# Two joined transformer blocks: narrower recurrence levels, query norms in pieces, and a pooling chain moved from GpSimd to VectorE

## The chip, the cores and the metric

The kernel runs on one NeuronCore of a Trainium2 chip. Its engines are TensorE (PE, matrix products), VectorE (DVE), ScalarE (ACT), GpSimd (POOL) and SyncE (SP, which here only issues DMAs). Each engine works through its own instruction list, and semaphores tie the lists together. The metric is the device time of one execution in microseconds; lower is better.

## The reference

Two models are computed, both with sequence 512 (S) and width 1024 (D). The first has two layers, each of mixer, cross-attention to a memory of 256 rows, and convolutional FFN. The even mixer joins a retention half and a gated recurrence half (HGRN2); the odd one is a dilated attention. The second has two equal layers of three parallel branches (attention with forget gates, short convolution, window pooling), gated and summed, and an FFN.

```python
# recurrence of the even mixer, per chunk (HGRN2)
cum = jnp.cumsum(lfn, axis=2)
w = jnp.exp(jnp.where(causal, cum[:, :, :, None, :] - cum[:, :, None, :, :], -jnp.inf))
scores = jnp.sum(qn[:, :, :, None, :] * kn[:, :, None, :, :] * w, axis=-1)
...
# cross-attention: both q and the memory's keys are normalised per head
q = _rms(_split_heads(h @ w_q, XA_HEADS), q_norm_g)
mk = _rms(_split_heads(mk, XA_HEADS), k_norm_g)
p = jax.nn.softmax(jnp.einsum('bhqd,bhkd->bhqk', q, mk) * (XA_HD ** -0.5), axis=-1)
o = jnp.einsum('bhqk,bhkd->bhqd', p, mv)
...
# pooling branch of the second model, windows 2, 4, 8, 16, one group of 64 channels each
cs = jnp.cumsum(uf, axis=1)
groups.append((csg - lagged) / counts - uf[:, :, sl])
out = jnp.einsum('bsgc,gcd->bsgd', d, w_grp).reshape(Bsz, S, D_MODEL)
```

## The kernel before

Activations stay in SBUF, transposed: 128 channels on the partitions, 512 positions along the row. Weights stream from HBM in units of 128x2048 floats (`raw`, two buffers, SP's queue). So that f32 weights can go through the PE fast and yet precisely, ACT writes a rounded copy of each unit, `wH` (L1197), and DVE the rest, `wL` = raw - wH (`split`, L1614). Activations are split likewise into `hH` and `hL`. Every product is then three matmuls (`passes`, L443): hH by wH, hL by wH, hH by wL. PE waits for `wl_ready`, SP may refill `raw` after it.

PE's work is counted in jobs: two PSUM tiles of `G` (four banks, so two jobs are open at a time). `job_done` tells DVE or ACT to read one, `job_free` gives the banks back. `psS` and `psT` (two banks each) serve scores, statistics and transposes. Nothing is scheduled at run time: the order on each engine is written out by hand, and each list blocks at its first unmet semaphore. DVE therefore is a strict queue in which weight splits, softmax rows and reads of finished jobs alternate.

What the change touches, by place:

- The recurrence levels (PE L782, DVE L2121 to L2140). The triangle of scores within a chunk is built in levels. At each level and for each of four heads PE multiplies keys by 512 query columns into psS; at level 0 DVE multiplies by a mask (L2137), at levels 1 to 5 it lets `copy_predicated` (L2140) take those entries that belong to the level, which all lie in the later half of each block. `grow` (L2121, L2122) prepares the next level's operands.
- The memory (ACT L1213 squares, PE L494 sums). Before each cross-attention ACT issues a DMA of the memory and directly waits for it, squares it and the residual stream in 128x512 pieces, and PE sums the squares over channels with a vector of ones.
- Cross-attention (PE L982, L989; DVE L2237 to L2275). Four query jobs are projected; after the last of them the squared queries of all four heads are summed (L499, L503), DVE copies 16 columns of sums out of PSUM (L1657), POOL raises them to -1/2 (L2511, 128x16) and 16 score rows start. A row: scores on PE, row maximum on DVE (L1821), times the norm (L2273), exponential on ACT (L1482), division on DVE, transpose and second product on PE.
- Dilated attention (PE L916, L933, L946; DVE L1821, L2186, L2213). 32 rows with value projections between them; `value_half` reads a projected tile and then splits the next weight unit (L1614).
- Second model's attention (PE L1080, L1089, L1116; DVE L2333, L2336, L1821, L2427, L2428). 32 rows in 16 pairs. Between them PE projects values, conv and pooling inputs; their squares and sums (L506) and DVE's reads (L2364, L2370, L2375) lie in the same lists. POOL meanwhile builds the window sums (L2587 to L2599) from position s=12 on. Four pool jobs follow at its end, each read by DVE (L2449) after a gate job (L1726).

`s_` and `d` below count the rows and the pairs of rows on which the three engines' lists are aligned.

## Time and profile before

| | us |
|---|---|
| median of 3 runs | 3182.88 (3181.28 to 3187.2) |
| profiled execution, device time | 3179.84 |
| its span (first to last instruction) | 3178.0 |
| PE busy | 3118.1 |
| DVE busy | 1584.6 |
| ACT busy | 1076.7 |
| POOL busy | 281.8 |
| mean granted PE clock | 0.992 |

A busy share is an average over stages. "Idle before" in a row is the time in which that engine did nothing before the instruction, with the engine and line that ended it behind the arrow. The ends of matmuls are modelled, so that durations of neighbouring matmul rows overlap; the distance of their starts is their cost.

### The profile page before, as it was taken

How to read it: one execution, taken by the hardware profiler on the slowest of the kernel's cores; microseconds unless marked ns; L12 is line 12 of the kernel's file. 1: busy time of each engine (PE TensorE's matmuls, PEld its weight loads, DVE VectorE, ACT ScalarE, POOL GpSimd, SP SyncE). 2: the span in 40 equal slices, each digit the busy share in tenths (PEclk: the TensorE clock that was granted, in tenths of full speed). 3: DMA queues.
4: the chain of work that ended last, by engine and by line, in shares of the span. 5: the costliest groups of instructions: out<-in, count | busy, mean ns of one | idle time of the engine just before them, and what ended most of it. 6: DMA issues, size and time to landing. Idle time of an engine off the chain costs nothing.

```text
span 3178.0 us, 38774 instructions
## 1 busy us (share of the span) xinstructions
PE 3118.1 (98%) x15548; PEld 2603.7 (82%) x15548; DVE 1584.6 (50%) x1852; ACT 1076.7 (34%) x1167; POOL 281.8 (9%) x161
## 2 busy tenths in 40 slices
PE   9999999999999899999999999999999999999998
PEld 7798988888889798888888778888888777888887
DVE  7574545554325554455435754544334765444433
ACT  3223334443223443444323332333322332233322
POOL 0002100110000020010001200111000200100100
PEclk9999999999999999999999999999999999999999
DMA  4411412222321131222233122222222222222223
GB/s 168 112 54 67 146 40 93 92 100 104 123 97 67 42 145 54 80 94 104 94 110 109 54 93 93 93 96 100 95 106 92 90 74 100 93 93 96 99 103 112
DMA packets 47721, 299.92 MB, mean 94 GB/s; under 512 B 7091, under 2 KB 7347, under 8 KB 13284
## 3 DMA queue, kind: packets, MB, share of 16 engines
q1 hardware_dynamic: 42480, 288.01, 25.7%
q10 hardware_dynamic: 5108, 10.02, 1.4%
q8 instruction: 98, 1.61, 0.2%
q14 instruction: 35, 0.29, 0.0%
HBM read 293.26 MB, written 4.75 MB: 94 GB/s over the span
## 4 chain that ended last, share of the span: by engine, by line
PE 90%; DVE 5%; ACT 2%; issue 2%; DMA 0%; POOL 0%; DVEq 0%; ACTq 0%; SPq 0%
PE G L443 82%; ACT wH L1197 1%; DVE wL L1614 1%; PE psS L782 1%; DVE mxt L1821 1%; PE psS L503 1%; PE psS L982 1%; PE G L989 1%; DVE ws L2336 1%; PE psS L1080 1%; PE G L1089 1%; DVE ws L2333 0%; PE psT L535 0%; PE psT L1116 0%; PE G L1007 0%
## 5 line engine op out<-in xcount | busy, mean ns | idle before, releaser
L443 PE MATMUL G<-hH,wH 128*128 128x512 f32 x2560 | 1019.9, 398 | 20.4 <-DVE ws L2364 5.7
L443 PE MATMUL G<-hH,wL 128*128 128x512 f32 x2560 | 1001.9, 391 | 0.0
L443 PE MATMUL G<-hL,wH 128*128 128x512 f32 x2560 | 1001.0, 391 | 0.0
L1614 DVE TENSOR_TENSOR wL<-raw,wH 128x2048 fp32r<-128x2048 f32 x265 | 637.5, 2406 | 647.3 <-ACT wH L1197 646.9
L443 PE MATMUL G<-wsr,wH 128*128 128x512 f32 (+1 forms) x2528 | 750.7, 380 | 1.4 <-DVE wsr L2202 0.9
L1197 ACT ACTIVATE wH<-raw 128x2048 fp32r<-128x2048 f32 x265 | 505.5, 1908 | 587.7 <-PE G L443 567.8
L443 PEld LDWEIGHTS G<-hH,wH 128*128 128x128 f32 x2560 | 483.6, 189 | 136.8 <-issue 17.6
L443 PEld LDWEIGHTS G<-hH,wL 128*128 128x128 f32 x2560 | 482.9, 189 | 103.2
L443 PEld LDWEIGHTS G<-hL,wH 128*128 128x128 f32 x2560 | 483.7, 189 | 99.5 <-issue 2.2
L443 PEld LDWEIGHTS G<-wsr,wH 128*128 128x128 f32 x2528 | 466.2, 189 | 94.8 <-DVE wsr L2202 1.8
L443 PE MATMUL G<-wsr,wL 128*128 128x512 f32 (+1 forms) x1264 | 479.0, 379 | 0.0
L443 PEld LDWEIGHTS G<-wsr,wL 128*128 128x128 f32 x1264 | 238.2, 188 | 44.6
L2533 POOL TENSOR_TENSOR wsr<-sq,wsr 128x1024 f32 x44 | 105.8, 2405 | 841.0 <-ACT wsr L1314 841.0
L2511 POOL TENSOR_TENSOR rsb<-ms,neghalf 128x4 f32<-128x4 f32 (+4 forms) x21 | 37.6, 1790 | 1144.4 <-DVE ms L1657 983.0
L1314 ACT ACTIVATE wsr<-sq 128x1024 f32 x44 | 46.7, 1061 | 231.5 <-DVE sq L1844 231.5
L1283 ACT ACTIVATE ws<-ws,mxt 128x128 f32<-128x128 f32 (+3 forms) x96 | 54.0, 563 | 206.7 <-DVE mxt L1821 206.1
L1768 DVE TENSOR_TENSOR x<-x,G 128x1024 f32<-128x1024 f32 x39 | 47.6, 1221 | 150.2 <-PE G L443 150.2
L443 PE MATMUL G<-wH,hH 128*128 128x256 f32 x384 | 112.1, 292 | 0.0
L443 PE MATMUL G<-wL,hH 128*128 128x256 f32 x384 | 108.6, 283 | 0.0
L443 PE MATMUL G<-wH,hL 128*128 128x256 f32 x384 | 108.5, 283 | 0.0
L1726 DVE TENSOR_TENSOR sq<-G,hmask 128x1024 f32<-128x1024 f32 x44 | 53.7, 1221 | 90.3 <-PE G L443 90.1
L1726 DVE TENSOR_TENSOR tn<-G,hmask 128x1024 f32<-128x1024 f32 x44 | 53.9, 1225 | 86.9 <-PE G L443 86.2
(275 smaller groups left out, 2570.2 us busy)
## 6 DMA issues: line engine op xcount, KB each, us to landing
raw<-in_units SPq DMA_DIRECT2D x265, 1024.0 KB, 4.8
ws<-bias_rows SPq DMA_DIRECT2D x2, 1536.0 KB, 14.9
bias_rows<-ws ACTq DMA_DIRECT2D x1, 2560.0 KB
x<-in_x SPq DMA_DIRECT2D x4, 512.0 KB, 7.4
ws<-in_mem ACTq DMA_DIRECT2D x2, 1024.0 KB, 5.0
ws<-bias_rows ACTq DMA_DIRECT2D x1, 2048.0 KB, 8.2
out_x<-x SPq DMA_DIRECT2D x4, 512.0 KB, 7.9
ws<-in_decay ACTq DMA_DIRECT2D x1, 1280.0 KB, 8.0
```

What stands on the lines that cost most here:

```text
L443: mm = pe.matmul(o, mv if swap else wt, wt if swap else mv, start=first and n == 0, stop=last and n == 2)
L503: mm = pe.matmul(st[:, col:col + 1], lhs, ones[:, 0:1], start=True, stop=True)
L782: mm = pe.matmul(psS[:, n % 2, o:o + w], k_[:, ks:ks + P], q_[:, qs:qs + w], start=True, stop=True)
L982: mm = pe.matmul(psS[:, r % 2, 0:M], ws[:, XQ + 2 * h + t, qt * P:qt * P + P], kx[:, 2 * h + t, :], start=(t == 0), stop=(t == 1))
L1197: activation(wH[:, g.p, :], raw[:, g.p, :], ACT.Copy).then_inc(wh_ready, 1)
L1283: return activation(p_, p_, ACT.Exp, bias=mxt[:, r % 4:r % 4 + 1], accum_out=den[:, r % 4:r % 4 + 1])
L1314: activation(aH[:, bass.ds(i * 2, 2), :], sq[:, 1], ACT.Copy).then_inc(ffn_h, 1)
L1614: V.tensor_tensor(wL[:, g.p, :], raw[:, g.p, :], wH[:, g.p, :].bitcast(F32), ALU.subtract)\
L1726: V.tensor_tensor(dst, g, rb_pair, ALU.mult).then_inc(job_free, 1)
L1768: V.tensor_tensor(x[:, 2 * jj:2 * jj + 2, :], x[:, 2 * jj:2 * jj + 2, :], g, ALU.add)\
L2511: W.tensor_tensor(dst[:, 0:cols], ms[:, 0:cols], neghalf[:].to_broadcast([P, cols]), ALU.pow)\
L2533: W.tensor_tensor(aL[:, bass.ds(i * 2, 2), :], sq[:, 1], aH[:, bass.ds(i * 2, 2), :].bitcast(F32), ALU.subtract).then_inc(ffn_ready, 1)
```

## The change

1. Recurrence. At levels 1 to 5 PE reads only the later half of each block's query columns, so 80 matmuls have 64 columns in place of 128 (128 for 256 in pairs), and DVE's `copy_predicated` moves 256 elements a row with strides in place of 512. The weight split that stood before level 0 is cut into four of 128x512 and put behind the four heads of level 1.
2. Memory. ACT issues the first memory DMA after its copies for the recurrence's last level, the second at row 20 of the dilated attention.
3. Cross-attention, both layers. The query norm is in four pieces of 4 columns (`query_norm`), so POOL raises 128x4 four times. Key scaling of the fourth head, the fourth query read, two of the norms and a weight split move from before the rows to between rows 0 and 4; the fourth sum goes to a `G` bank after score 1. ACT loads its table for the exponential in the third query step, and its rounding of one unit moves to row 3.
4. Dilated attention. Three weight splits move two rows down.
5. Second model, both layers. The window sums move from POOL to DVE, in six pieces at s=17, 19, 21, 23, 25 and 27 (`pooled`), with the final low parts between two gate jobs (`pooled_low`). The second half-statistics move from s=10 to s=13 and into another bank. The second and third pool job write to psS and psT, idle by then, and the weight splits stand after the first and the last pool read.

On DVE, at the recurrence's levels 0 and 1. Before:

```order
L1614 TENSOR_TENSOR wL<-raw,wH 128x2048 [waits wh_ready]
L2137 TENSOR_TENSOR ws<-psS,hmask 128x512 [waits hs_done] x4
L2121 TENSOR_TENSOR ws<-ws 128x64x4 [waits hz_ready,hs_done]
L2122 TENSOR_TENSOR ws<-ws 128x64x4
L2140 COPY_PREDICATED ws<-hmask,psS 128x512 [waits hm_ready]
```

and now, where L2173 is the old L2137, L2157 and L2158 `grow`, L2182 the narrower copy and L2144 a piece of the split:

```order
L2173 TENSOR_TENSOR ws<-psS,hmask 128x512 [waits hs_done] x4
L2157 TENSOR_TENSOR ws<-ws 128x64x4 [waits hz_ready,hs_done]
L2158 TENSOR_TENSOR ws<-ws 128x64x4
L2182 COPY_PREDICATED ws<-hmask,psS 128x64x4 [waits hm_ready]
L2144 TENSOR_TENSOR wL<-raw,wH 128x512 [waits wh_ready]
```

The split of 2048 columns has left the place ahead of the mask products and comes in quarters behind each head of level 1.

On DVE, from the last query job to the second row of a cross-attention. Before:

```order
L2258 TENSOR_SCALAR ws<-G,gqk 128x512 [waits sq_ready,job_done]
L2258 TENSOR_SCALAR ws<-G,gqk 128x512
L1614 TENSOR_TENSOR wL<-raw,wH 128x2048 [waits wh_ready]
L2265 TENSOR_TENSOR ws<-ws,psT 128x512 [waits rb_ready]
L1657 TENSOR_SCALAR ms<-psS 128x16 [waits sq_used]
L1821 TENSOR_REDUCE mxt<-psS 128x1 [waits s_done,rs_ready]
L2273 TENSOR_TENSOR mxt<-mxt,rsq 128x1 [waits dve_chain]
```

and now, where L2308 scales keys, L2315 copies sums out for POOL, L1846 and L2336 are a row's maximum and its norm, and L2302 reads queries:

```order
L2308 TENSOR_TENSOR ws<-ws,psT 128x512 [waits rb_ready]
L2315 TENSOR_SCALAR ms<-psS 128x4 [waits sq_used]
L1846 TENSOR_REDUCE mxt<-psS 128x1 [waits rs_ready,s_done]
L2336 TENSOR_TENSOR mxt<-mxt,rsq 128x1 [waits dve_chain]
L2308 TENSOR_TENSOR ws<-ws,psT 128x512 [waits rb_ready]
L1846 TENSOR_REDUCE mxt<-psS 128x1 [waits s_done]
L2336 TENSOR_TENSOR mxt<-mxt,rsq 128x1 [waits dve_chain]
L1835 RECIPROCAL rden<-den 128x1 [waits p_exp]
L1836 TENSOR_SCALAR ws<-ws,rden 128x256 [waits dve_chain]
L2315 TENSOR_SCALAR ms<-G 128x4 [waits sq_used]
```

The first row stands ahead of the fourth head's keys, queries and split; these come later, one to a row.

On DVE, at the end of the second model's attention, gates and pool jobs. Before:

```order
L1726 TENSOR_TENSOR ws<-G,hmask 128x1024 [waits job_done]
...
L1614 TENSOR_TENSOR wL<-raw,wH 128x2048 [waits wh_ready]
...
L1726 TENSOR_TENSOR ws<-G,hmask 128x1024 [waits job_done]
...
L2449 SCALAR_TENSOR_TENSOR ws<-G,pc,ws 128x512 [waits act_read]
L2449 SCALAR_TENSOR_TENSOR ws<-G,pc,ws 128x512
```

and now, where L1750 reads a gate, L2530 makes the low parts of the window sums and L2568 reads a pool job:

```order
L1638 TENSOR_TENSOR wL<-raw,wH 128x2048 [waits wh_ready]
L2530 TENSOR_TENSOR wsr<-sq,wsr 64x1024 [waits pdh_ready]
L2530 TENSOR_TENSOR wsr<-sq,wsr 64x1024
...
L1750 TENSOR_TENSOR ws<-G,hmask 128x1024 [waits job_done]
...
L2568 SCALAR_TENSOR_TENSOR ws<-psS,pc,ws 128x512 [waits act_read]
L2568 SCALAR_TENSOR_TENSOR ws<-psS,pc,ws 128x512
...
L2568 SCALAR_TENSOR_TENSOR ws<-psT,pc,ws 128x512 [waits act_read]
L2568 SCALAR_TENSOR_TENSOR ws<-psT,pc,ws 128x512
```

POOL's two last instructions of the window sums have become DVE's, and two pool reads come from psS and psT.

The diff, cut:

```diff
@@ attention of block 1, PE
-                pe.wait_ge(ms_ready, c.stat.v)
+                pe.wait_ge(ms_ready, keys_read + 2)
+                last_query = c.job.v + 2
                 for s_ in range(rows + PV_LAG):
                     if s_ < rows:
+                        if s_ == 12:
+                            pe.wait_ge(last_ready, l + 1)
+                            pe.wait_ge(job_free, last_query)
                         wait(pe, scores_read, c.row.v + (s_ - 1))
                         score(s_).then_inc(s_done, 1)
+                    if s_ == 1:
+                        stats("pair", 3, st=G[:, c.job.p * 2 + 1, :])
...
@@ recurrence, PE and DVE
+                                if 0 < lev < 6:
+                                    o, w, q = o // 2, w // 2, blocks(q, 2 ** (lev + 1))[1]
...
-                    step(inputs(1))
+                    step(inputs(1), unit=False)
+                    def split_part(q):
+                        at = slice(q * 512, q * 512 + 512)
+                        ins = V.tensor_tensor(wL[:, g.p, at], raw[:, g.p, at], wH[:, g.p, at].bitcast(F32), ALU.subtract)
...
+                                    b = psS[:, n % 2, 0:256].rearrange("p (k n l) -> p k n l", k=4, l=2 ** (lev + 1))
+                                    ins = V.copy_predicated(d, mask, b)
+                            if lev == 1:
+                                split_part(h)
@@ memory, ACT
-                    act.dma_start(memt[mem], a["mem"]).then_inc(mem_in, 16)
                     act.wait_ge(mem_in, 16 * (mem + 1))
...
+                    act.dma_start(memt[0], a["mem"]).then_inc(mem_in, 16)
                     step()
...
+                        elif s_ == 20:
+                            act.dma_start(memt[1], a["mem"]).then_inc(mem_in, 16)
@@ cross-attention, DVE
+                def between(s_):
+                    if s_ == 0:
+                        dve.wait_ge(rb_ready, c.bc.v)
+                        key_scale(3).then_inc(last_ready, 1)
+                    elif s_ == 1:
+                        query_norm(2)
+                    elif s_ == 2:
+                        step(queries(3), unit=False)
+                    elif s_ == 3:
+                        query_norm(3)
+                    elif s_ == 4:
+                        split()
+                        c.sq.off += 4
@@ second model, PE
-                    elif s_ == 10:
+                    elif s_ == 9:
+                        key_norm()
+                    elif s_ == 11:
                         pe.wait_ge(kn_read, (c.lay.v - 2) * 2 - 1)
-                        stats("half", 0, npairs=1, st=G[:, 3, :])
-                    elif s_ in (9, 11):
                         key_norm()
+                    elif s_ == 13:
+                        pe.wait_ge(pv_free, c.pv.v + 1)
+                        stats("half", 0, npairs=1, st=G[:, 1, :])
...
-                for jj in range(4):
-                    take_job()
+                for jj, bank in enumerate((None, psS, psT, None)):
+                    if bank is None:
+                        take_job()
...
+                    else:
+                        mm.then_inc(pooled_done, 1)
@@ second model, DVE
-                    elif s_ == 11:
-                        rstd_part(G[:, 3, :])
                     elif s_ == 12:
                         half_keys(1)
                         half_scaled(1, PX_)
+                    elif s_ == 15:
                         rstd_part_scaled(rsq[:, 16:32])
+                    elif s_ in (17, 19, 21, 23, 25, 27):
+                        pooled((s_ - 17) // 2)
...
+                def window(dst, src, lag):
+                    c.link(V.tensor_tensor(dst[:, :, lag:S], src[:, :, lag:S], src[:, :, 0:S - lag], ALU.add))
+                    c.link(V.tensor_copy(dst[:, :, 0:lag], src[:, :, 0:lag]))
+                def pooled(n):
+                    if n == 0:
+                        dve.wait_ge(pinv_in, (c.lay.v - 2) * 16)
+                        window(pa, u, 1)
...
+                    else:
+                        c.link(V.tensor_tensor(start, start, ws[rows, PINV:PINV + 2, 0:16], ALU.mult))
+                        V.tensor_tensor(start, start, u[rows, :, 0:16], ALU.subtract)
+                        for i, width in enumerate(widths):
+                            ins = V.scalar_tensor_tensor(t[rows, i, 16:S], t[rows, i, 16:S], 1.0 / width, u[rows, i, 16:S],
+                                                         ALU.mult, ALU.subtract)
@@ POOL
-                rstd(rsq, 16)
+                for j in range(4):
+                    rstd(rsq, ST, ST * j)
...
-                    c.link(W.tensor_tensor(dst[:, :, lag:S], src[:, :, lag:S], src[:, :, 0:S - lag], ALU.add))
...
-                W.tensor_tensor(wsr[64:P, PL:PL + 2, :], pb[64:P], wsr[64:P, PX_:PX_ + 2, :].bitcast(F32), ALU.subtract)\
-                    .then_inc(pdl_ready, 1)
```

## Rows read from the trace of the kernel before

**Rows 1.** The page: span, PE's busy time, and the chain that ended last.

```profile
span 3178.0 us, 38774 instructions
...
PE 3118.1 (98%) x15548; PEld 2603.7 (82%) x15548; DVE 1584.6 (50%) x1852; ACT 1076.7 (34%) x1167; POOL 281.8 (9%) x161
...
PE 90%; DVE 5%; ACT 2%; issue 2%; DMA 0%; POOL 0%; DVEq 0%; ACTq 0%; SPq 0%
```

**Rows 2.** PE's waits: engine, line <- releaser: us in total, times, longest us.

```profile
PE G L443 <- DVE ws L2364: 5.7, 3, 2.0
PE psS L916 <- DVE mxt L1821: 4.7, 3, 2.9
PE G L443 <- DVE ws L2370: 4.5, 2, 2.2
PE psS L494 <- ACT sq L1213: 4.3, 2, 2.9
PE G L506 <- DVE ws L2375: 4.0, 2, 2.0
PE G L443 <- DVE ws L2449: 3.7, 2, 1.9
...
PE psS L982 <- DVE ws L2265: 2.8, 1, 2.8
...
PE psS L782 <- DVE ws L2137: 1.9, 1, 1.9
```

**Rows 3.** Timeline (start us, us, what, xcount, [idle before]): DVE and PE at the recurrence.

```profile
201.51 2.29 DVE L1614 TENSOR_TENSOR wL<-raw,wH 128x2048 fp32r<-128x2048 f32 x1 [0.36 <-ACT wH L1197]
...
204.55 2.02 PE L782 MATMUL psS<-ws 128*128 128x128 f32 x16 [1.93 <-DVE ws L2137]
...
262.56 1.95 PE L503 MATMUL psS<-ones,sq 128*128 128x1 f32 x16 [0.73 <-ACT sq L1213]
```

**Rows 4.** Timeline: ACT and PE at the second memory transfer.

```profile
1085.08 1.15 ACT L1213 ACTIVATE sq<-ws 128x512 f32<-128x512 f32 x2 [4.57 <-DMA ws<-in_mem]
...
1085.86 4.92 PE L494 MATMUL psS<-ones,sq 128*128 128x1 f32 x32 [2.90 <-ACT sq L1213]
```

**Rows 5.** Timeline: start of the first cross-attention, and a 128x4 power elsewhere.

```profile
423.46 2.90 POOL L2511 TENSOR_TENSOR rsq<-ms,neghalf 128x16 f32<-128x16 f32 x1 [45.92 <-DVE ms L1657]
...
423.53 3.75 PE L982 MATMUL psS<-ws 128*128 128x256 f32 x8 [2.95 <-DVE ms L1657]
...
1317.84 1.01 POOL L2511 TENSOR_TENSOR rsb<-ms,neghalf 128x4 f32<-128x4 f32 x1 [87.22 <-DVE ms L1657]
```

**Rows 6.** Timeline: DVE in the dilated attention.

```profile
1041.59 2.29 DVE L1614 TENSOR_TENSOR wL<-raw,wH 128x2048 fp32r<-128x2048 f32 x1 [1.25 <-ACT wH L1197]
```

**Rows 7.** Windows: length, busy us (xcount) of PE, PEld, PEclk, DMA; L443 alone.

```profile
292.00:296.00 4.00, 4.00 (x10) 3.13 (x11) 0.50 0.02 4
297.00:301.00 4.00, 4.00 (x19) 3.03 (x18) 1.00 0.63 246
```

**Rows 8.** Windows of all: PE, PEld, DVE, ACT, POOL, then PEclk, DMA, GB/s.

```profile
422.50:429.30 6.80, 5.30 (x12) 3.77 (x13) 2.48 (x9) 1.31 (x4) 2.90 (x1) 0.50 0.42 157
2600.30:2603.60 3.30, 3.30 (x10) 2.56 (x9) 0.04 (x1) 0.00 (x0) 0.00 (x0) 0.50 0.00 0
```

**Rows 9.** Windows: DVE alone, then PEclk, DMA, GB/s; the last two L2336 alone.

```profile
1724.00:1766.00 42.00, 26.04 (x62) 0.96 0.28 105
1774.00:1796.00 22.00, 21.39 (x29) 1.00 0.15 49
1700.00:1774.00 74.00, 4.09 (x14) 0.98 0.29 86
1774.00:1792.00 18.00, 5.16 (x4) 1.00 0.18 59
```

**Rows 10.** Timeline: POOL in the second model's attention, DVE at the gates.

```profile
1789.28 2.41 POOL L2594 TENSOR_TENSOR sq<-sq,ws 64x1024 f32<-64x1024 f32 x1
...
1886.57 1.22 DVE L1726 TENSOR_TENSOR ws<-G,hmask 128x1024 f32<-128x1024 f32 x1 [6.48 <-PE G L443]
```

More of the change, by code:

```diff
@@ L974, in _ @@
                     if j:
-                        stats("pair", j - 1, added=7 * l + 4 + j)
+                        pe.wait_ge(ms_ready, c.stat.v)
+                        stats("pair", j - 1, npairs=j, st=st if j < 3 else G[:, c.job.p * 2, :],
+                              added=7 * l + 4 + j)
                 c.nrm.off += 8
-                stats("pair", 3)
                 def score(r):
@@ L992, in pv @@
                     return mm
-                attention(16, lambda r: 2, lambda r: ws[:, XP + r % 4, 0:M], score, pv, 1, p_exp)
+                attention(16, lambda r: 2, lambda r: ws[:, XP + r % 4, 0:M], score, pv, 1, p_exp, l, keys_read)
                 residual(xo_op, operand=stored(c.job.off))
@@ L1272, in attention @@
                         copy(r).then_inc(pt_ready, 1)
-                    if between and s_ == rows - LAG:
+                    if between and s_ == 3:
                         between()
@@ L1477, in _ @@
                 for j in range(4):
-                    step(square)
+                    step(square, unit=j < 3)
+                    if j == 2:
+                        activation(tick[:, 2 + l:3 + l], neghalf[:], ACT.Exp)
                 xprobs = lambda r: ws[:, XP + r % 4, 0:M]
@@ L1583, in _ @@
                 gates(2)
-                for jj in range(4):
-                    step(unit=jj == 3)
+                c.job.off += 1
+                step()
                 act.wait_ge(cv_ready, c.lay.v - 3)
@@ L1790, in residual, with attention @@
                         norm(lambda k: memt[mem][:, k, :], lambda k: col1(mem, "mem", k), M)
-            def attention(rows, probs, row, out_h, out_l, per_job):
+            def attention(rows, probs, row, out_h, out_l, per_job, between):
                 n_out = 0
@@ L2197, in read @@
                             return ins
-                        half_step(read, unit=t == 1)
+                        half_step(read)
                     def head_out(h):
@@ L2251, in _, with queries, read @@
                 columns(0, 2)
-                for j in range(4):
-                    if j < 3:
-                        columns(2 * j + 2, 2)
-                    def queries(g):
+                def queries(j):
+                    def read(g):
                         for t in range(2):
@@ L2260, in queries, with key_scale, query_norm @@
                         ins.then_inc(job_free, 1)
[L2261 to L2266 removed]
+                    return squared(j, read)
+                def key_scale(j):
+                    return V.tensor_tensor(kx[:, 2 * j:2 * j + 2, :], kx[:, 2 * j:2 * j + 2, :],
+                                           psT[:, (first + j) % 2, 0:M].unsqueeze(1).to_broadcast([P, 2, M]), ALU.mult)
+                def query_norm(j):
+                    dve.wait_ge(sq_used, c.sq.v + j + 1)
+                    at = st if j < 2 else G[:, pv_slot * 2 + j - 2, :]
+                    V.tensor_scalar(ms[:, 4 * j:4 * j + 4], at[:, 4 * j:4 * j + 4], 1.0 / 256, EPS, ALU.mult, ALU.add)\
+                        .then_inc(ms_ready, 1)
+                    c.stat.off += 1
+                norms = c.stat.v
+                pv_slot = c.job.p
+                for j in range(3):
+                    columns(2 * j + 2, 2)
+                    step(queries(j))
+                    add_pair(j, S)
+                    dve.wait_ge(rb_ready, c.bc.v - 1)
+                    ins = key_scale(j)
+                    if j:
+                        query_norm(j - 1)
                 ins.then_inc(kv_ready, 1)
[L2268 removed]
                 xprobs = lambda r: ws[:, XP + r % 4, 0:M]
                 def row(r):
+                    if r % 4 == 0:
+                        dve.wait_ge(rs_ready, norms + r // 4 + 1)
                     c.link(row_max(r, psS[:, r % 2, 0:M]))
@@ L2440, in gates, with pools, read @@
                         step(scaled(ws[:, GATE + 2 * jj:GATE + 2 * jj + 2, :]), unit=first == 0 or jj == 2)
+                        if first and jj == 2:
+                            pooled_low()
                 gates(2)
-                for jj in range(4):
-                    def pools(g):
+                def pools(jj):
+                    def read(g):
                         dve.wait_ge(act_read, c.ar.v + 1)
@@ L2450, in pools @@
                                                          ws[:, GATE + 2 * jj + t, :], ALU.mult, ALU.mult)
-                        ins.then_inc(job_free, 1)
-                    step(pools, unit=jj in (1, 3))
+                        return ins
+                    return read
+                step(lambda g: pools(0)(g).then_inc(job_free, 1))
+                for jj, bank in ((1, psS), (2, psT)):
+                    dve.wait_ge(pooled_done, (c.lay.v - 4) * 2 + jj)
+                    pools(jj)(bank)
+                step(lambda g: pools(3)(g).then_inc(job_free, 1))
                 z, y = ws[:, CC:CC + 2, :], ws[:, CX:CX + 2, :]
```

113 lines of the change are left out of this document (63 added, 50 removed).

## The prediction

> **What bounds the kernel now.** I read the page first. PE is busy for 3118.1 of 3178.0 us, and the chain that ended last lies on PE for 90% of the span and on DVE for 5% [rows 1]. So PE bounds it, and there are two ways to gain: fewer PE cycles, or less of the 59.9 us in which PE is idle (3178.0 - 3118.1). Work taken off another engine gains only where PE waits for it. PE's waits, by line, come second: they are short, and the engine that ends them is nearly always DVE [rows 2]. DVE as a whole is half idle, so a wait means that its list is late in a place, not that it has too much to do. Third I read the timeline at each of these waits for what stands ahead of the late instruction, and last the windows, for the granted clock behind the waits. A wait can cost more than its own length: in 292 to 296 us PE ran 10 matmul records of L443 at a granted clock of 0.50, that is 1.2 GHz, and in 297 to 301 us 19 at 1.00, 2.4 GHz [rows 7]. A stretch of 3.4 us at the lower level therefore costs about 1.6 us (3.4 x (1 - 10/19)). Such stretches follow PE waits of 2 us or more, as after the wait on L2370 at 2600 us, or the one of 2.95 us at 423.53 [rows 5, 8]; not all such waits have one.
>
> **The change part by part.**
>
> *Recurrence.* PE waits 1.93 us at 204.55 for the mask product L2137, in front of which DVE makes a weight split of 2.29 us [rows 3]. The split moves behind it, in quarters between heads of level 1, where PE has its own filler matmuls. The wait goes: -2.0. The halved columns are the larger-looking edit: 80 matmuls, 160 records. But 16 records with 128 columns took 2.02 us, and 16 with a single column 1.95 us [rows 3]. The column count costs nothing down at this size; what is paid is a floor per record of some 0.12 us, the load of the stationary operand. So I put 0 for it. The other bound is that half of the time of 64 columns goes, 160 x 0.06 = 9.6 us. The narrower copy_predicated leaves DVE more air where PE does not wait; 0.
>
> The page "TensorE: Matmul & The Clock Gate" of the Trainium skill gives two rules for this. Its section "Back-to-back issue gap" has N/2.4 + 2.5 ns for the isolated gap, 55.8 ns for 128 columns, by which halving saves 27 ns each, an estimated 4 us in all. Its section "LDWEIGHTS (loading the stationary operand)" has P/1.2 ns, 107 ns for 128 columns of weights, whatever is streamed, by which nothing is saved. The two rows side by side agree with the second.
>
> *Memory.* Twice PE waits for squares of a memory whose DMA ACT issues only there: 4.3 us together, the second 2.90 us [rows 2, 4]; ACT itself stands 4.57 us for the transfer. Issued 32 us and more before its use, the transfer is done by then and ACT can make its first two squares in that idle time. Both waits go: -4.3. The 32 records themselves took 4.92 us, where 32 x 1.95/16 = 3.9 would do; the rest is ACT's squares, of which two are now ahead. -0.5 each, -1.0. Bounds for the part: -3 (a small wait for a first square stays) to -8.5 (the slow clock behind both goes too, 1.6 x 2). Value -5.3. ACT's queue is past nothing new: the issue stands behind copies that are long done when PE needs the next thing.
>
> *Cross-attention.* The waits are 2.95 us (423.53) and 2.8 us in the second layer [rows 2, 5], and behind the first the stretch 422.5 to 429.3 is at 0.50, with PE busy 5.30 of 6.80 us [rows 8]. At fault is a series: ACT's rounding, DVE's split, key scaling, sum copy, then POOL's 128x16 power of 2.90 us [rows 5], then the first row. With the power in pieces of 4 columns (1.01 us each, rows 5) and the fourth head out of the way, score 0 needs nothing late. But what left comes back between rows 0 and 4: queries 1.4 us, the split 2.29, and ACT's rounding at row 3, beside rows which DVE and ACT must make. I let about half of each 7 us (2.95 wait, 0.5 of a second wait, 3.4 of clock) remain: -3.5 per layer, -7.0. Bounds: -2 in all (the waits turn up at rows 3 to 6) to -12.
>
> The section "Who interferes with whom" of the Trainium skill's page "SBUF — State Buffer" speaks against this part: DVE operations with two SBUF inputs and GpSimd's share a port pair as an exclusive lock. Four powers in place of one then each may hold up a DVE row by an estimated 1.0 us, 4 us a layer at worst, which would leave about nothing of the part and end near 3148 us. The trace agrees that something of this kind exists: L2336 took 0.29 us alone and 1.29 us on average beside POOL's additions [rows 9]; that a power does it too no row here shows.
>
> *Dilated attention.* DVE stands 1.25 us for ACT's `wH`, then splits for 2.29 us, and only then makes the row for which PE waits 2.91 us at 1044.78; the same with 0.93 us at 1015.65: L916 has 4.7 us in three waits [rows 2, 6]. Two rows later `wH` is ready and the row goes first. Some 3.9 of the 4.7 go. PE's next need of that unit is later than the two rows. -3.9, bounds -2 and -5.
>
> *Second model.* Here is the most. The waits on L2364, L2370, L2375 and L2449 sum to 5.7 + 4.5 + 4.0 + 3.7 = 17.9 us [rows 2]. Why is DVE late in the first three? In 1724 to 1766 us it is busy for 26.04 of 42, in 1774 to 1796 us, while POOL builds window sums, for 21.39 of 22 [rows 9]. It does not do more there: L2336, a 128x128 addition, takes 4.09/14 = 0.29 us before, and 5.16/4 = 1.29 us beside POOL's long instructions of 2.41 us [rows 9, 10]. With these gone from POOL the stretching goes. L2375's wait is the statistics' place at s=10, which moves to where the bank is free. L2449's is the two job slots of the pool jobs, which the banks psS and psT double. I take all 17.9, and 0.9 for the slower restart behind them.
>
> What is added: DVE makes the sums itself. A window over two tiles has 128x1022 elements; the nearest row is the 128x1024 addition at 1.22 us [rows 10], so the pieces are about 1.3, 1.3, 0.75, 0.75 and 1.65, 1.65 us, 7.4 a layer against 22 us on POOL, and pooled_low at 2 x 1.2 lies in the 6.48 us of idle DVE time ahead of the gate [rows 10]. Per pair of rows DVE then has some 7.0 us to do in PE's 7.4 to 8.0. That fits closely: I put +0.5 per layer for the pair in which a 1.65 us piece follows a split, +1.0. Bounds: 0, and a case where each piece costs its POOL time, below. Last the clock: four stretches of 3.4 us at the lower level stand behind these waits (one is in rows 8): -1.6 x 4 = -6.4. Value of the part: -17.9 - 0.9 + 1.0 - 6.4 = -24.2; bounds -12 (half of the waits come back in other rows, clock stretches too) and -27.
>
> **Sum.** -2.0 - 5.3 - 7.0 - 3.9 - 24.2 = -42.4 us. The profiled execution had 3179.84 us, 1.84 over its span; that gives 3137.4. The median of the runs shown lies 3.0 us above the profiled one, so 3140.5 us.
>
> **The rivals.**
> - *Half is passed on.* A PE wait ended by DVE is often followed by one that DVE's next row would have had anyway, and DVE is left near full in the pairs of rows. Then the memory and recurrence waits go (-7), but the attentions give half: -13 to -16, and half of the clock stretches stay. About -21: 3162. For it: the many short waits in rows 2 that are not listed as large; against it: DVE's cause there, the stretching, has one source and that is removed.
> - *Columns do pay.* If the 0.12 us of a record is not a floor for 64 columns, 9.6 us more go: 3131. Against: the single-column row of 1.95 us.
> - *DVE becomes the bound, slower.* The window pieces work on 64 partitions and strided halves, and each link waits for the one before. If they take on DVE what they did on POOL (2.41 us for 64x1024, rows 10; some 22 us a layer, 3.7 a piece), a row pair with a piece needs 7.0 - 1.25 + 3.7 = 9.5 us in PE's 7.7. That is 1.8 x 12 = 22 us of new waits, and each of them can open a stretch at 0.50, 1.6 x 12 = 19. Against the 18.8 us of old waits the part then is at +22; with the cross-attention's -7 lost to the same lateness and -11 from the rest the execution has 3191 and the median 3194. It decides from a piece price of about 2.9 us, where 12 x 1.0 + 19 - 18.8 just outweighs those 11. Against: the 1.22 us row.
> - *Nothing happens.* The waits removed are replaced by equal ones, since PE's total is set elsewhere: 3183. Against: PE's chain at 90% has nothing else to be set by.
>
> **Chances.** Forecast 60%, half passed on 25%, columns 4%, nothing 6%, slower 5%. The range takes the forecast's own bounds, the second case and its spread: 3127 to 3166, its own range 3129 to 3152. Runs of this kernel differ by about 0.2%, 6.4 us, so that less is called no change. Faster 0.89, same 0.06, slower 0.05.
>
> **What would show it.** In the new profile the waits on L782, on L494 and on the first score of each cross-attention should be absent or under 0.5 us, records of L782 should still start as far apart as now, and the DVE rows at L2336 should all be at 0.29 us. PE busy should hardly change but for the clock stretches (3118 less about 7 to 10), and idle fall to some 25 us. I am wrong if PE waits for window pieces, if the addition on DVE takes much over 1.3 us, if stretches at 0.50 stay in the cross-attentions with waits at rows 3 to 6, or if the narrow matmuls come closer together.

## The result and the profile after

The changed kernel takes 3135.66 us (median, 3134.47 to 3136.43), the one before in the same runs 3185.04. The ratio is 0.9846, 95% interval 0.9829 to 0.9863: faster by 49 us, where 42 were forecast for the profiled pair and 3140.5 us for the median. The profiled executions are 3178.0 and 3132.7 us long, 45.3 apart; executions of the kernel before spread over 3179.4 to 3188.9, and its profiled one lay near the lower end.

The page of the changed kernel, to be held against [rows 1]:

```profile
span 3132.7 us, 38793 instructions
...
PE 3101.5 (99%) x15548; PEld 2594.6 (83%) x15548; DVE 1575.0 (50%) x1897; ACT 1076.0 (34%) x1169; POOL 237.5 (8%) x139
...
PE 91%; DVE 5%; ACT 2%; issue 2%; DMA 0%; DVEq 0%; ACTq 0%; POOL 0%; SPq 0%
```

PE executes the same 15548 records, yet is busy for 16.6 us less: that is nearly all the clock. Its idle time falls from 59.9 to 31.2 us, 28.7 less. The two make the 45.3. I searched both traces in steps of 3.4 us for a granted clock below 0.97. Leaving out the start and the end, 13 stretches of 3.4 us at 0.50 were there before (one at 265 us, two each at 289, 422, 1088 and 1224, four in the second model) and 3 are left (at 262, 287 and 1076). Ten of them at 1.6 us would be 16 us; but in the cross-attentions PE stood still for a part of them, 5.30 busy of 6.80 us in the first [rows 8] and 3.96 in the second:

```profile
1224.60:1231.40 6.80, 3.96 (x11) 2.76 (x10) 3.56 (x5) 0.13 (x2) 2.90 (x1) 0.50 0.43 154
```

So PE worked at 0.50 for 40.0 us before (nine whole stretches of 3.4, 5.3 and 4.0) and for 10.2 us now, and the difference of 29.8 us is worth 14.1 us (x 9/19, as in rows 7). The other 2.5 us are matmul records that follow each other closer, most of them at the pool jobs, as e8 shows below. Each of the three stretches that are left stands behind a series of records with a single column (L504 at 260 us, L495 at 283 and 1071 us), and PE had no wait over 1 us in the 9 us ahead of them.

PE's waits in the changed kernel, largest first, with those that answer to [rows 2]:

```profile
PE psS L995 <- ACT ws L1506: 5.1, 10, 1.0
PE G L444 <- DVE wL L1638: 3.3, 5, 1.2
PE psS L927 <- DVE mxt L1846: 2.8, 3, 1.4
...
PE G L444 <- DVE ws L2447: 1.3, 2, 0.6
```

None is over 2 us in the stages that the change touches. The waits for L2364, L2375 and L2449 (now L2441, L2452, L2568) are gone, and L2370 (now L2447) has 1.3 us left of 4.5.

At the recurrence, against [rows 3], PE and DVE:

```profile
202.52 1.95 PE L794 MATMUL psS<-ws 128*128 128x128 f32 x16
205.70 1.89 PE L794 MATMUL psS<-ws 128*128 128x64 f32 x16
...
207.41 0.42 DVE L2182 COPY_PREDICATED ws<-hmask,psS 128x256 f32<-128x256 int32 x1
```

The wait of 1.93 us is absent. Sixteen records of 64 columns take 1.89 us, those of 128 took 1.95: halving the columns gives PE nothing. The copy, though, takes 0.42 us, where the kernel before has 0.75 for 512 elements.

At the second memory, against [rows 4], PE and ACT:

```profile
1071.10 3.63 PE L495 MATMUL psS<-ones,sq 128*128 128x1 f32 x32
...
1068.72 1.14 ACT L1233 ACTIVATE sq<-ws 128x512 f32<-128x512 f32 x2
```

ACT has its first two squares ready before PE comes, and 32 records take 3.63 us, not 4.92. That they took 4.92 was the clock and not ACT. In the kernel before, the same records alone in two windows (PE, PEld, PEclk, DMA, GB/s):

```profile
1085.90:1088.10 2.20, 2.20 (x21) 2.20 (x21) 1.00 0.00 0
1088.10:1090.60 2.50, 2.50 (x14) 2.50 (x13) 0.50 0.00 0
```

They follow at 112 ns until 1088.1 us and at 213 ns from there on, with no wait between any two.

At the start of the first cross-attention, against [rows 5]: two of POOL's pieces of the power, PE's scores, DVE's late query read and the division of a row, then the windows (PE, PEld, DVE, ACT, POOL, PEclk, DMA share, GB/s) that answer to [rows 8], the second with the records of before's 2600.3 us:

```profile
415.95 1.01 POOL L2636 TENSOR_TENSOR rsq<-ms,neghalf 128x4 f32<-128x4 f32 x1 [8.88 <-DVE ms L2315]
...
412.44 1.97 PE L995 MATMUL psS<-ws 128*128 128x256 f32 x8
...
420.77 1.13 PE L995 MATMUL psS<-ws 128*128 128x256 f32 x4 [0.96 <-ACT ws L1506]
...
418.10 1.40 DVE L2302 TENSOR_SCALAR ws<-G,gqk 128x512 f32<-128x512 f32 x2
...
420.64 1.01 POOL L2636 TENSOR_TENSOR rsq<-ms,neghalf 128x4 f32<-128x4 f32 x1 [3.69 <-DVE ms L2315]
...
420.14 0.35 DVE L1836 TENSOR_SCALAR ws<-ws,rden 128x256 f32<-128x256 f32 x1
420.93 0.16 DVE L2336 TENSOR_TENSOR mxt<-mxt,rsq 128x1 f32<-128x1 f32 x1
421.19 0.35 DVE L1836 TENSOR_SCALAR ws<-ws,rden 128x256 f32<-128x256 f32 x1
```

```profile
414.00:420.80 6.80, 5.53 (x35) 4.59 (x34) 5.32 (x20) 2.70 (x9) 1.17 (x2) 1.00 0.00 0
2559.30:2562.60 3.30, 3.30 (x21) 2.80 (x20) 0.10 (x1) 0.26 (x1) 0.00 (x0) 1.00 0.00 0
```

Score 0 starts with no wait, small waits stand at rows 2 to 5 in its place (0.32, 0.96, 0.38 and 0.75 us in this layer), and the clock stays at 1.00 through both stretches. The division takes 0.35 us ahead of the piece of the power at 420.64 and inside it.

In the second model, against [rows 9] and [rows 10]: the 128x128 addition (now L2413) alone in a window (DVE busy, PEclk, DMA, GB/s), two kinds of window piece, PE's wait for a filler read there, and two reads of pool jobs in psS and psT.

```profile
1760.00:1800.00 40.00, 2.93 (x10) 1.00 0.15 54
```

```profile
1768.34 1.22 DVE L2502 TENSOR_TENSOR sq<-ws 128x1022 f32<-128x1022 f32 x1
...
1800.10 1.25 DVE L2522 SCALAR_TENSOR_TENSOR sq<-sq,ws 64x496 f32<-64x496 f32 x2
...
1791.15 0.50 PE L444 MATMUL G<-hH,wH 128*128 128x512 f32 x1 [0.64 <-DVE ws L2447]
...
1862.83 1.41 DVE L2568 SCALAR_TENSOR_TENSOR ws<-psS,pc,ws 128x512 f32<-128x512 f32 x2
1864.15 1.41 DVE L2568 SCALAR_TENSOR_TENSOR ws<-psT,pc,ws 128x512 f32<-128x512 f32 x2
```

The addition takes 0.29 us every time, the addition of a window piece 1.22 as in a gate's row.

### The profile page after: what moved, and what is told of

Same layout as the page of the kernel before. It is cut to its first block, busy times and chain, and to the rows that moved or that the text cites. A ratio compares the mean times of both kernels' runs of the same rounds, so it can differ in the third digit from the quotient of the medians.

```text
span 3132.7 us, 38793 instructions
## 1 busy us (share of the span) xinstructions
PE 3101.5 (99%) x15548; PEld 2594.6 (83%) x15548; DVE 1575.0 (50%) x1897; ACT 1076.0 (34%) x1169; POOL 237.5 (8%) x139
## 4 chain that ended last, share of the span: by engine, by line
PE 91%; DVE 5%; ACT 2%; issue 2%; DMA 0%; DVEq 0%; ACTq 0%; POOL 0%; SPq 0%
PE G L444 83%; ACT wH L1217 1%; DVE wL L1638 1%; PE psS L794 1%; DVE mxt L1846 1%; PE psS L504 1%; PE psS L995 0%; PE psS L1096 0%; PE G L1105 0%; PE G L1002 0%; DVE ws L2410 0%; PE psT L536 0%; PE psT L1132 0%; PE G L1020 0%; DVE ws L2229 0%
## 5 line engine op out<-in xcount | busy, mean ns | idle before, releaser
L1750 DVE TENSOR_TENSOR sq<-G,hmask 128x1024 f32<-128x1024 f32 x44 | 53.7, 1221 | 90.3 <-PE G L444 90.1
L1750 DVE TENSOR_TENSOR tn<-G,hmask 128x1024 f32<-128x1024 f32 x44 | 53.9, 1224 | 86.9 <-PE G L444 86.3
```

The costliest lines, as they stand in the source:

```text
L1750: V.tensor_tensor(dst, g, rb_pair, ALU.mult).then_inc(job_free, 1)
```

## The experiments

The first eight undo one part each in the changed kernel. "Median more" is against its 3135.66 us, "span more" against its 3132.7 us. A single execution differs from the next by up to 1.6 us for each stretch at half clock that appears or not, so differences under 2 us in these two columns say nothing. The last column leaves out the stretches elsewhere: it is by how much more the start of the same matmul record is late at the end of the part's own stage than at its start, against the changed kernel's trace (stages from 200 to 257 us, 278 to 298 and 1063 to 1085, 412 to 438 and 1204 to 1230, 998 to 1063, and from 1230 us to the end).

| kernel | median | median more | span more | in its stage |
|---|---|---|---|---|
| e1 window sums on GpSimd | 3148.98 | +13.3 | +13.6 | +12.1 |
| e2 cross-attentions as before | 3143.68 | +8.0 | +10.3 | +7.9 |
| e3 memory DMAs as before | 3144.91 | +9.3 | +9.7 | +9.2 |
| e4 full columns | 3136.27 | +0.6 | +1.7 | +1.7 |
| e5 split ahead of level 0 | 3138.73 | +3.1 | +3.3 | +2.1 |
| e6 dilated splits as before | 3138.32 | +2.7 | +1.6 | +2.0 |
| e7 statistics at s=10 | 3146.30 | +10.6 | +10.5 | +9.3 |
| e8 pool jobs in two slots | 3145.01 | +9.4 | +10.8 | +9.3 |
| e9 heavier window pieces | 3167.68 | +32.0 | +32.0 | +30.5 |
| e10 idle GpSimd additions | 3150.23 | +14.6 | +14.8 | +14.6 |
| e12 quarters and halves | 3132.64 | -3.0 | -1.2 | -4.3 |

The eight parts sum to 57 us by their medians, against 49 for all together, and to 54 in their stages, against 45 for the pair of traces.

**e1, window sums back on GpSimd.** The POOL block of the kernel before is put back and `pooled` and `pooled_low` go:

```diff
-                    elif s_ in (17, 19, 21, 23, 25, 27):
-                        pooled((s_ - 17) // 2)
...
+                    c.link(W.tensor_tensor(dst[:, :, lag:S], src[:, :, lag:S], src[:, :, 0:S - lag], ALU.add))
```

> The changed kernel, with the window sums of the second model given back to GpSimd (all other edits kept, GpSimd starts after its power for the second half statistics). Theory (GpSimd's long additions stretch VectorE's, and that makes VectorE late): the 128x128 causal additions show over 1 us beside them again in place of 0.29, PE waits again for the reads of filler jobs, and the time is 10 to 16 us above the changed kernel, two or three stretches at half clock included. Rival (VectorE was late by the order of its list alone, which stays changed): the additions are stretched but PE hardly waits, 0 to 3 us. Second rival (work on VectorE is what now costs): 1 to 3 us faster than the changed kernel, since 15 us of work leave VectorE.

```profile
PE G L444 <- DVE ws L2441: 5.7, 4, 2.2
...
PE G L444 <- DVE ws L2447: 4.5, 2, 2.2
```

The waits came back at their old size, and the time at +13.3, 12.1 of the profiled 13.6 in the second model. The theory holds and both rivals fall, but for what exactly GpSimd does, e10 is needed, since here VectorE's list is changed too.

**e10, GpSimd busy for nobody.** After its power, GpSimd makes seven additions into a free tile:

```diff
+                for _ in range(7):
+                    c.link(W.tensor_tensor(tn[:], x[:, 0:2, :], x[:, 2:4, :], ALU.add))
```

> The changed kernel, where GpSimd after its power in the second model's attention makes seven 128x1024 additions of the residual stream into a free tile, which nobody reads; VectorE's list is untouched. Theory (GpSimd's long additions stretch VectorE's): the causal additions and the divisions beside them take 1 us and more in place of 0.29, window pieces too, and PE waits: 5 to 15 us. Rival (in the kernel before VectorE was late by its list and GpSimd's part was its own chain being late): no change in VectorE's rows and 0 us.

The timeline of POOL and DVE:

```profile
1752.24 2.90 POOL L2636 TENSOR_TENSOR rsq<-ms,neghalf 128x16 f32<-128x16 f32 x1 [25.14 <-DVE ms L1724]
1755.10 17.23 POOL L2705 TENSOR_TENSOR tn<-x 128x1024 f32<-128x1024 f32 x7
...
1753.22 0.29 DVE L2413 TENSOR_TENSOR ws<-ws,causal 128x128 f32<-128x128 f32 x1
...
1762.68 0.35 DVE L2410 SCALAR_TENSOR_TENSOR ws<-psS,rsq,ws 128x128 f32<-128x128 f32 x1
1763.07 2.08 DVE L2413 TENSOR_TENSOR ws<-ws,causal 128x128 f32<-128x128 f32 x1
1765.18 0.29 DVE L1846 TENSOR_REDUCE mxt<-ws 128x1 f32<-128x128 f32 x1
...
1768.05 1.94 DVE L2545 TENSOR_SCALAR ws<-ws,rden 128x128 f32<-128x128 f32 x1
```

PE then waits 10.4 us for L2441, and the clock falls in both layers. The cost is +14.6 us with VectorE's list untouched: GpSimd's additions alone do it. They stretch an addition of two SBUF tiles from 0.29 to 2.08 us and a scaling from SBUF to SBUF from 0.29 to 1.94, but neither the operation that reads PSUM nor the reduction; and the power, 2.90 us long, stretches nothing: the addition at 1753.22 lies inside it, like three more VectorE instructions.

**e11, that part alone on the kernel before.** The same hunks of the diff applied to it, nothing else.

> The kernel before with one part of the change alone: the window sums on VectorE in place of GpSimd. Theory: its waits on the filler reads (5.7 and 4.5 us in all) go and so do stretches at half clock behind them, those on the statistics (4.0) and the pool jobs (3.7) stay: 10 to 15 us faster than before. Rival (the parts need each other, the gain is only there with the statistics moved too): 0 to 5 us.

The median is 3174.43 against 3185.32 for the kernel before, ratio 0.9967 (0.9956 to 0.9977): 10.9 us faster, within the theory's 10 to 15. (Its profiled span is only 5.6 us under that of before. In the second model its trace is 10.0 us shorter; in the other stages, which it leaves alone, 4.4 us longer, with 12 stretches at half clock where the kernel before had 9.) The waits on the statistics (4.0) and the pool jobs (3.7) stay as they were. The rival falls; the part stands alone.

**e9, the price at which it would have been slower.** Each piece carries two additions more:

```diff
+                    for _ in range(2):
+                        c.link(V.tensor_tensor(tn[:, :, 1:S], x[:, 0:2, 1:S], x[:, 2:4, 0:S - 1], ALU.add))
```

> The changed kernel, where each of the six window pieces on VectorE carries two more additions of 128x1022, linked one to the next, whose sums nobody reads: 1.4 us a piece becomes 3.8 us, the price of the rival that ends slower than before. By that rival's working 1.8 us of new waits for each of 12 pieces and a stretch at half clock with many of them: +22 to +41 us against the changed kernel. By the slack that the changed trace shows (VectorE idle 2.0 to 5.9 us ahead of three of the four splits of that stretch, waiting for the rounded copy): much of it is taken up there, +5 to +15.

PE's waits, and the timeline of DVE and PE at the third piece and behind it:

```profile
PE G L444 <- DVE ws L2447: 16.9, 11, 2.0
PE psS L1096 <- DVE mxt L1846: 7.3, 9, 2.7
```

```profile
1789.01 2.29 DVE L1638 TENSOR_TENSOR wL<-raw,wH 128x2048 fp32r<-128x2048 f32 x1 [0.44 <-ACT wH L1217]
1791.21 2.47 DVE L2508 TENSOR_TENSOR tn<-x 128x1022 f32<-128x1022 f32 x2
...
1788.62 0.50 PE L444 MATMUL G<-hH,wH 128*128 128x512 f32 x1 [2.03 <-DVE ws L2447]
1798.29 0.49 PE L1096 MATMUL psS<-ws 64*128 64x128 f32 x4 [2.67 <-DVE mxt L1846]
```

+32.0 us, as the rival's working had it (+22 to +41) and not as the slack would (+5 to +15). VectorE's idle time is ahead of a split, where it stands for ScalarE's rounding, and the piece comes behind the split: it can't use it. So each pair is nearly full, and most of the 2.5 us more goes straight to PE. Even so the kernel stays 17 us under the one before, where my rival had 3194 us. PE's two waits grew by 21.6 us, which is the rival's 1.8 us for each of 12 pieces; but five stretches at half clock stand in the second model's trace and not 12, so that the pieces cost 30.5 us and not 41. What they stand against was larger than the rival had it: 25.9 us in the second model and not 18.8, and 17.9 us in the other stages and not 11, as the cross-attentions kept their gain.

**e2, cross-attentions as before.** All of part 3 undone, for example:

```diff
-                for j in range(4):
-                    rstd(rsq, ST, ST * j)
+                rstd(rsq, 16)
```

> The changed kernel with both cross-attentions as before (one power of 128x16, fourth head ahead of the rows). Theory: each gets back its wait of 2.8 to 3.0 us before the first score and the stretch of 6.8 us at half clock, and loses the small waits of rows 2 to 5; 3.5 us each, 7 in all, 5 to 9. Rival (four powers each hold up a VectorE row by their 1.0 us): no more than 2 us.

```profile
PE psS L985 <- DVE ms L1669: 3.0, 1, 3.0
PE psS L985 <- DVE ws L2299: 2.9, 1, 2.9
```

+8.0 us: the theory's size, and the rival falls. The power of 1.01 us at 415.95 lies where VectorE idles in any case, and the one at 420.64 beside two of its instructions, which it leaves at 0.16 and 0.35 us. Of the +10.3 us of the span 2.4 lie in other stages, most of it in one more stretch at half clock each at 1057 and at 1078 us.

**e3, memory DMAs as before.**

```diff
+                    act.dma_start(memt[mem], a["mem"]).then_inc(mem_in, 16)
                     act.wait_ge(mem_in, 16 * (mem + 1))
```

> The changed kernel with the two memory DMAs where they were, directly in front of ScalarE's wait. Theory: waits of 1.4 and 2.9 us return, with 0.5 us of spacing each and one more stretch of 3.4 us at half clock behind each: +5.3 without the clock, +8.5 with it. Rival (the transfer was hidden by the sums anyway): under 2 us.

PE's wait, and a window at the second memory (PE busy, PEclk, DMA, GB/s):

```profile
PE psS L495 <- ACT sq L1233: 3.9, 2, 2.5
```

```profile
1084.60:1088.00 3.40, 3.40 (x10) 0.50 0.00 0
```

+9.3 us, where waits and spacing alone would be 5.3. The waits are 3.9 us, and nearly all the rest is the clock: behind the waits it stays low for two and three stretches, where the changed kernel has one each, 4.8 us more. The spacing of my sum is a part of this clock, as the two windows of L494 above show.

**e4, all columns, and e5, the split in front.** e4 takes back the halving on PE and VectorE, e5 the quarters:

```diff
-                                if 0 < lev < 6:
-                                    o, w, q = o // 2, w // 2, blocks(q, 2 ** (lev + 1))[1]
```

```diff
-                    step(inputs(1), unit=False)
+                    step(inputs(1))
```

> The changed kernel with all 128 columns in the recurrence's levels 1 to 5, on PE and on VectorE. Theory (a record of up to 128 columns costs its weight load): 0, at most 1 us. Rival (columns count): +4 by 27 ns for each of 160 records, +9.6 by half their time.

> The changed kernel with the one whole weight split of 2.29 us back ahead of level 0 of the recurrence, in place of four quarters in level 1. Theory: the wait of 1.9 us before the second head's products returns, +2.0. Rival (the level is paced by PE's weight loads, and its filler hides a wait): under 0.5 us.

In e4, PE and DVE at level 1:

```profile
209.54 1.13 PE L791 MATMUL psS<-ws 128*128 128x128 f32 x8 [0.30 <-DVE ws L2174]
...
208.69 0.72 DVE L2174 COPY_PREDICATED ws<-hmask,psS 128x512 f32<-128x512 int32 x1
```

e4's +0.6 us rules out 9.6 and 4 us for the columns. Its trace shows one effect that I had put at 0: with full copies a head of level 1 costs VectorE 0.41 + 0.41 + 0.72 + 0.67 less overlaps, 1.89 us from one to the next, and two heads 3.8 us, where PE passes two in 3.17. Two waits follow, at 209.54 (0.30) and 213.32 (0.36), two short ones at 238 and 241 us, and the levels run 1.7 us longer. With the narrow copy a head costs 1.60. e5's wait of 1.93 us is back at 204.19 and its time is +3.1: the theory, since 2.1 us of it lie in the recurrence.

**e6, dilated splits as before.** The three `split` calls back at their rows.

> The changed kernel with the three weight splits of the dilated attention two rows up, where they were. Theory: 3.9 us back, of it 1.5 to 2 at the wait that was 2.91 us and is 1.43 now, as VectorE again stands for the rounded copy. Rival (the splits only moved the lateness to later rows): 0 to 1.5 us.

Its L927 (the L916 of before) waits 4.7 us in place of 2.8, 1.9 us more. The median is +2.7, the span +1.6, and both hold stretches elsewhere; in its own stage the part is worth 2.0 us: half of the forecast 3.9, and a little above the rival's 1.5.

**e7, statistics at s=10.**

```diff
+                    elif s_ == 10:
...
+                        pe.wait_ge(kn_read, (c.lay.v - 2) * 2 - 1)
+                        stats("half", 0, npairs=1, st=G[:, 3, :])
```

> The changed kernel with the second half statistics of the second model back at position 10 in bank G3. Theory: the wait of 2.0 us for VectorE's key scaling comes back in each layer, +4, and a stretch at half clock behind it, +3.2: 4 to 7. Rival (it waited only since GpSimd had made VectorE late): under 1 us, since the sums are elsewhere now.

```profile
1740.55 2.08 PE L507 MATMUL G<-halves,sq 128*128 128x2 f32 x16 [1.99 <-DVE ws L2449]
```

```profile
2485.40:2488.80 3.40, 3.40 (x9) 0.50 0.00 0
```

The waits (4.0 us) are back though GpSimd is idle, so the cause was the place in the list; the rival falls. +10.6 us is more than my 4 to 7: behind the waits stand three stretches at half clock in the two layers, 4.8 us, and waits and stretches make 8.8 of the 9.3 us of its stage. The other 1.2 us of the span lie ahead of it, mostly in one stretch more at 262 us, which this part does not touch.

**e8, pool jobs in two slots.** `bank` is None for all four, splits behind the second and fourth read.

> The changed kernel with all four pool jobs in the two slots of G, and weight splits after the second and fourth read. Theory: the wait of 1.9 us for the read of a pool job returns in each layer, +3.7. Rival (it was the split between the reads and not the number of banks): in this kernel both are undone, so the trace must show which instruction VectorE is in while PE waits; if the split, its time of 2.3 us lies wholly inside the wait.

DVE and PE at the third read:

```profile
1863.76 2.28 DVE L1634 TENSOR_TENSOR wL<-raw,wH 128x2048 fp32r<-128x2048 f32 x1
1865.96 2.72 DVE L2564 SCALAR_TENSOR_TENSOR ws<-G,pc,ws 128x512 f32<-128x512 f32 x4
...
1867.41 0.51 PE L444 MATMUL G<-hH,wH 128*128 128x512 f32 x1 [1.86 <-DVE ws L2564]
```

The wait of 1.86 us ends with the first of the reads that stand behind the split of 2.28. PE's wait begins at 1865.55, so that only 0.5 us of the split lie inside it and not the whole, by which I would have told the rival. With four banks and the split elsewhere it is gone; which of the two does it was not tried. The waits make 3.7 us. The records of the pool jobs themselves take 0.9 us a layer more: at each change of job in G two records follow at some 340 ns, where they follow at 227 ns with psS and psT. One stretch at half clock stands behind the wait of the second layer, 1.6 us. That makes 7.2 of the 9.3 us of its stage; 1.5 more are a stretch at 2494 us, ahead of that layer's pool jobs, and outside the stage stand one more each at 1054 and 1078 us, which this part does not touch. So the part is worth some 7 us and not the median's 9.4, and the 3.7 that I expected were its waits alone.

**e12, further in the same direction.** ScalarE's rounding and VectorE's split in quarters on rows of their own in the cross-attentions, halves in the dilated one, three window pieces ahead of the split they stood behind:

```diff
+                    elif s_ in (7, 8, 10, 11):
+                        split_some((7, 8, 10, 11).index(s_), 4)
...
+                    elif s_ == 20:
+                        half_scaled(1, CX, unit=False)
+                        pooled(2)
+                        split()
```

> The changed kernel taken further: in the cross-attentions ScalarE's rounding is in quarters at rows 3 to 6, VectorE's split in quarters at rows 7, 8, 10 and 11 and the fourth query read in two halves; in the dilated attention the splits are in halves on two rows; in the second model three window pieces stand between a filler read and its split, where VectorE waits for the rounded copy. If the waits that are left come from these whole instructions and from standing for the rounded copy: 2 to 3 us from the cross-attentions, 1 to 1.5 from the dilated one, 1.3 from the second model, in all 4 to 6 us below the changed kernel. If they are only moved from row to row: within 1.5 us of it.

```profile
PE psS L927 <- DVE mxt L1867: 1.6, 3, 0.9
...
PE psS L995 <- ACT ws L1517: 1.5, 6, 0.3
```

The waits at cross-attention rows fell from 5.1 to 1.5 us, those of the dilated one from 2.8 to 1.6, and the one for L2447 is gone. The median of 3132.64 (3131.01 to 3134.26) does not overlap with the changed kernel's 3134.47 to 3136.43: 3.0 us less, short of the 4 to 6 expected. The stages say more than the median: 3.8 us less in the two cross-attentions, 1.2 in the second model and 0.5 in the dilated attention up to 1045 us, 5.4 in all and within the 4 to 6. In the profiled execution three stretches at half clock that the changed kernel's has not, at 262, 1053 and 1075 us, take most of it back; e1 and e8, which leave these places alone, have them too.

## Why the prediction was right

The two traces have the same matmuls in nearly the same order, so the difference in the start of the same record, before and after a stage, gives each part (the stages are those of the table above):

| part | forecast | pair of traces | undone (median) | undone (in its stage) |
|---|---|---|---|---|
| recurrence | -2.0 | -2.7 | 3.1, 0.6 | 2.1, 1.7 |
| memory | -5.3 | -8.0 | 9.3 | 9.2 |
| cross-attention | -7.0 | -6.7 | 8.0 | 7.9 |
| dilated | -3.9 | -2.1 | 2.7 | 2.0 |
| second model | -24.2 | -25.9 | 13.3, 10.6, 9.4 | 12.1, 9.3, 9.3 |

They sum to the 45.4 us of the traces: between the stages nothing was won or lost.

*Recurrence.* Right in the wait and in the 0 for PE's columns: both 4 and 9.6 us for the columns fell with e4, and the floor per record held. Wrong in "The narrower copy_predicated leaves DVE more air where PE does not wait; 0": without it PE would wait at level 1, as e4's waits show, and its own stage is 1.7 us longer.

*Memory.* Right in the waits (4.3 us, gone) and undersized: 5.3 against 8.0 and 9.2. I had left the clock behind the waits out of the value and only in the bound of -8.5. And my term of -1.0 for ACT's squares was a misreading: the 32 records took 4.92 us because the clock fell while they ran (112 ns apart, then 213), so I had counted a piece of the clock under another name. Of the two stretches behind each wait one stays without the wait.

*Cross-attention.* The size of -7.0 was right by luck, a guess at "half". Its make-up: waits of 2.95 and 2.8 went, small waits grew from 1.6 us in four pieces to 5.1 in ten, and the clock of two stretches in each layer came back whole, 4.4 us in all, since PE was busy for 5.3 and 4.0 of 6.8 us in them. The exclusive lock did not show: at 420.64 the division and the norm of a row kept their 0.35 and 0.16 us inside a power of 1.01 us, and the two-input addition at 1753.22 in e10 took 0.29 us inside one of 2.90 us. By the Trainium skill's "SBUF — State Buffer", section "Who interferes with whom", a VectorE instruction with two SBUF inputs and a GpSimd instruction that reads SBUF contend for a port pair that is an exclusive lock. That fits GpSimd's additions in e10 (0.29 to 2.08 us) and not its power.

*Dilated.* The order of the list was at fault, as forecast (e6), but the term is nearly twice what it gave, 3.9 against 2.1. The waits on L916 fell from 4.7 to 2.8 us: the row behind the moved split still waits 1.43 us, and one of 0.47 us came at 1001 us.

*Second model.* Right in cause (e1, e10, e11), in price of the pieces (7.9 us a layer in the trace, 7.4 forecast) and in the new waits (0.64 and 0.63 us against 0.5 a layer). The 0.9 us for a slower restart no row shows; at the pool jobs records that follow closer gave 1.9 us (e8), which I had not seen. The slower rival's mechanism is real (e9), but the row of 1.22 us that spoke against it decided.

What was mis-sized most is the clock. Of 45.3 us the waits gave 28.7, the clock 14.1 and the closer records 2.5. My sum of 42.4 held 30.7 for waits, 6.4 for the clock in the second model and 3.4 in the cross-attentions, 9.8, and 1.9 for spacing and restart. So the clock gave 4.3 more, the records 0.6 more and the waits 2.0 less, and 2.9 of the 4.8 us between forecast and median come from there. The other 1.9 come from the 3.0 us added for the median over the profiled execution: the changed kernel's is only 1.2 over its own. Two of my signs show the same: PE's idle time fell to 31.2 us and not to 25, and its busy time by 16.6 and not by 7 to 10. Nor do the stretches only follow waits of 2 us or more, as I wrote: those of the kernel before at 265 and 289 us follow waits of 0.73 and 1.43 us.

## What to carry to other kernels

Where one engine is busy for 98%, read its waits by what stands ahead of the late instruction in the releaser's list, and look at the granted clock behind each wait: here the clock was worth half as much as the waits themselves. Where parts are small, compare the start of the same record before and after a stage, and not whole times, which hold stretches at half clock from elsewhere. Idle time of a helper engine can be used only by what stands ahead of the wait, not behind it. Long elementwise work on GpSimd was no free help: beside it, VectorE's SBUF-to-SBUF operations took up to eight times as long.

## What the runs showed of the hardware

- GpSimd's 128x1024 addition (2.4 us) stretches VectorE's two-input and scaling operations between SBUF tiles from 0.29 to 1.9 to 2.3 us. An operation with an operand in PSUM (0.35 us) and a reduction (0.29) beside it are untouched, and so are four VectorE instructions inside GpSimd's power of 128x16 (2.90 us in e10), one of them an addition of two SBUF tiles, and the norm and the division inside one of 128x4 (1.01 us).
- A matmul record with 64 columns starts the next one 55 ns later only at the head of a group, where one with 128 columns does it 108 ns later; the others follow at 111 ns, as with 128 columns and with one, and the last record of the group makes up for it (84 ns against 31), so that nothing is won. Those with 256 columns follow at 216 ns.
- Behind waits of PE of 2 to 3 us stand between none (1044.78 in the kernel before) and three stretches at half clock (e2 at 1214 us, e3 at 1078 us), and the three that the changed kernel keeps stand where no wait over 1 us is near. Each costs 1.6 us where PE works throughout it, less where PE waits: one at 1054 us in e1 costs the kernel 0.4 us. Profiled executions differ by up to three of them in stages that were not touched (e11).
